# Two-layer diffusion backbone on one core: attention of layer 0 started without a barrier behind its projection, pooled products spread over neighbouring steps

## The reference, cut to what matters

```python
def mixer_ab(h, hc, w_in, w_out, pool_w, pool_scale, sink, cos, sin, need_ctx):
    u, q, k, v = split_ab(h @ w_in)              # 512 pooled channels, 8 query heads, 2 key/value heads
    uc, qc, kc, vc = split_ab(hc @ w_in)
    q, k = apply_rope(q, cos, sin), apply_rope(k, cos, sin)
    a = windowed_latent_attention(q, k, v, kc, vc, sink)
    y = jnp.concatenate([pool_mix(u, pool_w, pool_scale), a], axis=-1) @ w_out
    ...
def pool_mix(u, w, scale):                       # windows 2, 4, 8, 16, one per group of 128 channels
    ...
    d = (pooled - uf).astype(u.dtype)
    y = jnp.einsum('btgc,gce->btge', d, w).reshape(B, T, POOL_CH)
    return y * scale
```

## Time and profile before

| | us |
|---|---|
| median of 3 runs | 1578.04 (1577.26 to 1580.77) |
| the profiled execution | 1582.88, its span 1580.8 |
| PE busy | 1473.0 (93% of the span) |
| DVE busy | 966.0 (61%) |
| ACT busy | 716.3 (45%) |
| POOL busy | 596.6 (38%) |
| chain that ended last, share of PE | 83% |

### The profile page before, as it was taken

How to read it: one execution, slowest core, us unless ns; L and a number is a source line. 1 busy time by engine, 2 the same in 40 slices (tenths; PEclk the granted TensorE clock), 3 DMA queues, 4 the chain that set the end, 5 groups by cost and what they waited for, 6 DMA issues and landing times.

```text
span 1580.8 us, 22196 instructions
## 1 busy us (share of the span) xinstructions
PE 1473.0 (93%) x7604; PEld 1200.9 (76%) x7604; DVE 966.0 (61%) x1478; ACT 716.3 (45%) x1230; POOL 596.6 (38%) x529
## 2 busy tenths in 40 slices
PE   4989798999999999999999698899999999999997
PEld 1877466787888888887888577678877888887886
DVE  2447588567787668843345567788876544445455
ACT  2332466644332333223343545487775554443453
POOL 2251354352232232322333532375552444443454
PEclk9999799999999999999999899899999999999999
DMA  8230750123554346311121112110003233332332
GB/s 339 55 101 0 256 199 28 26 83 105 162 173 133 107 146 186 111 62 60 56 74 60 50 52 90 44 41 1 1 1 93 68 93 106 93 93 80 95 96 102
DMA packets 129034, 147.06 MB, mean 93 GB/s; under 512 B 7284, under 2 KB 95608, under 8 KB 127936
## 3 DMA queue, kind: packets, MB, share of 16 engines
q1 hardware_dynamic: 128960, 146.07, 29.5%
HBM read 143.92 MB, written 2.14 MB: 92 GB/s over the span
## 4 chain that ended last, share of the span: by engine, by line
PE 83%; DVE 7%; ACT 3%; POOL 2%; DMA 2%; issue 2%; SPq 0%; DVEq 0%; POOLq 0%; ACTq 0%
PE ps L471 23%; PE ps L472 23%; PE ps L473 23%; PE ps L1428 4%; PE ps L1414 3%; PE ps L1439 2%; PE ps L1441 2%; DMA ada_w<-in_ada_w_dram 1%; DMA start_w<-in_ada_w_dram 1%; PE ps L924 1%; POOL w_lo L463 1%; PE ps L1330 1%; DVE hT_lo L803 1%; ACT prob L1468 1%; DVE hT_hi L801 1%
## 5 line engine op out<-in xcount | busy, mean ns | idle before, releaser
L463 POOL TENSOR_TENSOR w_lo<-raw,w_hi 128x1024 fp32r<-128x1024 f32 (+1 forms) x183 | 346.5, 1896 | 618.0 <-ACT w_hi L456 618.0
L471 PE MATMUL ps<-hT_hi,w_hi 128*128 128x512 f32 (+1 forms) x1096 | 387.8, 354 | 9.3 <-DVE hT_lo L803 5.1
L472 PE MATMUL ps<-hT_lo,w_hi 128*128 128x512 f32 (+1 forms) x1096 | 385.3, 352 | 0.0
L473 PE MATMUL ps<-hT_hi,w_lo 128*128 128x512 f32 (+1 forms) x1096 | 382.9, 349 | 0.0
L456 ACT ACTIVATE w_hi<-raw 128x1024 fp32r<-128x1024 f32 (+1 forms) x200 | 173.0, 866 | 196.8 <-PE ps L473 166.5
L471 PEld LDWEIGHTS ps<-hT_hi,w_hi 128*128 128x128 f32 x1096 | 207.4, 189 | 47.1 <-DVE hT_lo L803 5.7
L473 PEld LDWEIGHTS ps<-hT_hi,w_lo 128*128 128x128 f32 x1096 | 206.8, 189 | 28.7
L472 PEld LDWEIGHTS ps<-hT_lo,w_hi 128*128 128x128 f32 x1096 | 207.3, 189 | 26.9
L2299 DVE TENSOR_TENSOR g_lo<-act_g,g_hi 128x768 fp32r<-128x768 f32 (+1 forms) x82 | 103.8, 1273 | 149.4 <-ACT g_hi L2258 149.0
L471 PE MATMUL ps<-w_hi,g_hi 128*128 128x512 f32 x410 | 160.2, 391 | 5.0 <-DVE g_lo L2299 4.5
L473 PE MATMUL ps<-w_hi,g_lo 128*128 128x512 f32 x410 | 159.6, 389 | 0.0
(11 more groups left out here) (242 smaller groups left out, 2433.3 us busy)
## 6 DMA issues: line engine op xcount, KB each, us to landing
raw<-in_ffn_w_up_dram SPq DMA_DIRECT2D x84, 512.0 KB, 3.9
ada_w_up<-in_ada_w_dram SPq DMA_DIRECT2D x48, 512.0 KB, 4.2
raw<-in_ffn_w_down_dram SPq DMA_DIRECT2D x84, 256.0 KB, 2.6
ada_w<-in_ada_w_dram SPq DMA_DIRECT2D x32, 512.0 KB, 4.9
start_w<-in_ada_w_dram SPq DMA_DIRECT2D x8, 1024.0 KB, 10.9
raw<-in_c_w_qkv_dram SPq DMA_DIRECT2D x12, 512.0 KB, 3.8
raw<-in_ab_w_in_dram SPq DMA_DIRECT2D x8, 512.0 KB, 5.0
raw<-in_ab_w_out_dram SPq DMA_DIRECT2D x8, 512.0 KB, 3.7
```

Of the source, the lines that this page charges most:

```text
L463: by.tensor_tensor(w_lo[:, slot, 0:width], raw[:, n % RAW, 0:width], w_hi[:, slot, 0:width].bitcast(F32), ALU.subtract).then_inc(lo_split, 1)
L471: nc.tensor.matmul(outp, s_hi, m_hi, start=first, stop=False, skip_group_check=True)
L472: nc.tensor.matmul(outp, s_hi, m_lo, start=False, stop=False, skip_group_check=True)
L473: return nc.tensor.matmul(outp, s_lo, m_hi, start=False, stop=last, skip_group_check=True)
```

## The change

1. The barrier between the two stages goes, on PE, ACT, DVE, POOL and SP. In its place stand the waits that the data need; SP waits for the last tile and for the fourth pooled product.
2. `pool_split` of windows 0 and 1 moves on DVE from behind tile 10 to behind tile 8, that of 2 and 3 from behind tile 11 to behind tile 10. On PE, products 0 and 1 move in front of the turn of tile 9. Scores S0 of group 0 go in front of the turn of tile 11, S1 behind it.
3. Products 2 and 3 become a step M in slot 0 of attention, their evictions a step m in slot 1. All A, H, P, Z, U, W and Y move two slots later (`POOL_FILLS`). A 0 also waits for the last pooled eviction.
4. d1 moves to memory that attention does not use at that time.

```diff
+POOL_FILLS = 2
...
-        at.setdefault(4 * (p // 3) + p % 3, []).append(("A", p, 0))
+        at.setdefault(POOL_FILLS + 4 * (p // 3) + p % 3, []).append(("A", p, 0))
...
-        at.setdefault(3, []).append(("H", 0, 0))
-        at.setdefault(7, []).append(("H", 1, 0))
+        at[0], at[1] = [("M", 2, 0), ("M", 3, 0)], [("m", 2, 0), ("m", 3, 0)]
+        at.setdefault(POOL_FILLS + 3, []).append(("H", 0, 0))
+        at.setdefault(POOL_FILLS + 7, []).append(("H", 1, 0))
...
+                        if l == 0 and n == len(tiles) - 2:
+                            pool_product(pe, 0)
+                            pool_product(pe, 1)
...
-            if l == 0:
-                pool_products((0, 1))
-            for late in range(n - TURN_LAG[l], n):
-                turn(late)
-            if l == 0:
-                pool_products((2, 3))
-            close(pe, "pe")
+            if l:
+                for late in range(n - TURN_LAG[l], n):
+                    turn(late)
+                close(pe, "pe")
+            return lambda: turn(n - 1)
...
+                        if l == 0 and n == len(tiles) - 1:
+                            pool_hi(act, 0)
...
-                if l == 0 and n == len(tiles) - 2:
+                if l == 0 and n == len(tiles) - 4:
                     pool_split(dve, 0)
                     pool_split(dve, 1)
+                if l == 0 and n == len(tiles) - 2:
+                    for f in (2, 3):
+                        dve.wait_ge(s("pool_mm"), f - 1)
+                        pool_split(dve, f)
             if l == 0:
-                for f in (2, 3):
-                    dve.wait_ge(s("pool_mm"), f - 1)
-                    pool_split(dve, f)
-                for f in range(4):
-                    pool_lo(dve, f)
-            close(dve, "dve")
+                pool_lo(dve, 0)
+            else:
+                close(dve, "dve")
...
-            after_phase(pe, before)
+            if l:
+                after_phase(pe, before)
...
+                    if kind == "M":
+                        pool_product(pe, g)
+                    elif kind == "A":
+                        if g == 0:
+                            pe.wait_ge(s("pool_out"), 16)
                         ada0_products(pe, g)
...
                     if h >= 2:
                         pe.wait_ge(s(f"exp_done{l}"), per * (h - 2) + 1)
+                    elif l == 0 and h == 0:
+                        pe.wait_ge(s("turned_read0"), rope_plan(0)[1][-2] - 2)
+                    elif l == 0:
+                        last_turn()
+                        pe.wait_ge(s("turned_read0"), rope_plan(0)[1][-1])
...
-                    after_phase(sp, 4)
+                    sp.wait_ge(s("acc_done0"), len(token_tiles(0)))
+                    sp.wait_ge(s("pool_mm"), 4)
                     ada0_sync(sp)
```

More of the change, by code:

```diff
@@ L976, in proj_tensor, with pool_product @@
                 m += 4
[L977 to L986, removed]
-            if l == 0:
-                pool_products((0, 1))
-            for late in range(n - TURN_LAG[l], n):
-                turn(late)
-            if l == 0:
-                pool_products((2, 3))
-            close(pe, "pe")
+            if l:
[3 more added lines that the diff above has]
+            return lambda: turn(n - 1)
+        def pool_product(pe, f):
+            pe.wait_ge(s("pool_d"), 2 * f + 2)
+            if f >= 2:
+                pe.wait_ge(s("pool_out"), 4 * (f - 1))
+            for v, (c0, w) in enumerate(STREAMS):
+                p0 = PADDED[v][0]
+                mm = mm3(bank(4 + 2 * (f % 2), 1024)[:, c0:c0 + w], pw_hi[:, f, :], pw_lo[:, f, :],
+                         d_hi[f % 2][:, p0:p0 + w], d_lo[f % 2][:, p0:p0 + w], True, True)
+            mm.then_inc(s("pool_mm"), 1)
         def proj_prefetch(l):
@@ L1092, in proj_scalar, with pool_hi @@
                     m += 1
+            if l == 0:
+                pool_hi(act, 1)
             for late in range(n - TURN_LAG[l], n):
                 read_turned(late)
-            if l == 0:
-                for f in range(4):
-                    act.wait_ge(s("pool_mm"), f + 1)
-                    for v, (c0, w) in enumerate(STREAMS):
-                        nc.scalar.activation(hT_hi[:, f, c0:c0 + w], bank(4 + 2 * (f % 2), 1024)[:, c0:c0 + w],
-                                             ACT.Copy, scale=cols[:, 48 + f:49 + f]).then_inc(s("pool_hi"), 1)
-            close(act, "act")
+            if l:
+                close(act, "act")
+        def pool_hi(act, f):
+            act.wait_ge(s("pool_mm"), f + 1)
+            for v, (c0, w) in enumerate(STREAMS):
+                nc.scalar.activation(hT_hi[:, f, c0:c0 + w], bank(4 + 2 * (f % 2), 1024)[:, c0:c0 + w],
+                                     ACT.Copy, scale=cols[:, 48 + f:49 + f]).then_inc(s("pool_hi"), 1)
         DIFFERENCE_AFTER = (0, 2, 7, 9)
@@ L1372, in ada0_columns, with attn_tensor @@
                                         ALU.mult).then_inc(s("gates_made0"), 1)
-        def attn_tensor(pe, l, before):
+        def attn_tensor(pe, l, before, last_turn=None):
             groups, steps, first = attn_setup(l)
@@ L1447, in attn_scalar @@
             groups, steps, first = attn_setup(l)
-            after_phase(act, before)
+            if l:
+                after_phase(act, before)
             for kind, g, i in steps:
-                if kind in "APZUWYHzu":
-                    if kind == "H":
+                if kind in "APZUWYHzuMm":
+                    if kind == "m":
+                        pool_hi(act, g)
+                    elif kind == "H":
                         out_split_hi(act, l, g)
@@ L1504, in attn_vector @@
             steps = outputs_first(steps)
-            after_phase(dve, before)
+            if l:
+                after_phase(dve, before)
+            else:
+                dve.wait_ge(s("qk_steps0"), rope_plan(0)[0][-1])
             nden = 2 if l == 0 else 1
@@ L1527, in attn_vector @@
                 if kind == "S":
+                    if l == 0 and h == 1:
+                        pool_lo(dve, 1)
                     dve.wait_ge(s(f"scores{l}"), h + 1)
@@ L2400, in _ @@
             for l in range(2):
-                b = 5 * l
+                b = 4 * l
                 norm_vector(dve, f"mix{l}", b + 2)
```

37 lines of the change are left out of this document (21 added, 16 removed).

## The result

The changed kernel takes 1582.71 us (median of 8 runs, 1579.63 to 1585.98), the kernel before beside it 1577.99. The ratio is 1.0027, with a 95% interval of 1.0015 to 1.0039: slower by about 4.3 us by the ratio (4.7 by the two medians), where 1576.7 was forecast. Run again word for word it took 1581.36 us, ratio 1.0017 (1.0004 to 1.0031). The loss is small, but there.

The account below looks back on a forecast made before the run. PE sets the pace to about 234 us, DVE for some 24 us, then PE; SP's ada_w request limits attention's start. 3.0 + 3.2 - 4.35 - 0.5 = 1.35 us less: 1576.7 us, range 1571 to 1582.

Parts of the forecast that it names:

- term 4: From group 6 to the end of attention: waits that go and come sum to 0.5 us lost.
- term 2: From the start of A 0 to the first turn of group 1: 3.2 us more won.
- The bound of 4.5 us lost: Groups 6 to the end: worst case, none of three old waits goes and both new ones come.
- a sign of being wrong: The forecast is wrong if groups 6 to 11 take over 3 us less or more than before.
- the end pays: Rival, end of attention: all three old waits go, 3.4 us won there, 1572.8 us in all; chance 0.23.
- Term 1: Start of attention: SP's ada_w loads go at 160.5 in place of 163.5, 3.0 us earlier.
- my first rival: The clock falls to half at the last projection turn: 2.3 us later, net 1 us lost, 1579.0; chance 0.15.
- Term 3: Ada pairs side by side: PE waits 1.3 us at A 5, A 8, A 11, A 14; 4.35 us lost.
- Slow load: Rival at A 5, A 8, A 11, A 14: tiles land after 6.2 us, net 8.25 lost, 1586.3; chance 0.12.
- POOL's splits: Rival at H 0 and H 1: PE pays 1.69 us twice, net 2.0 lost, 1580.1; chance 0.05.
- Renamed barrier: Rival, start of attention: SP still waits for four products and goes no earlier, 1579.7 us; chance 0.03.
- The offset: Whole kernel: median of runs 4.8 us below the profiled execution, subtracted to give the base of 1578.04 us.

Follow-up runs that it names:

- unpaired: The changed kernel with only the ada pairs moved so that no two stand side by side: 1574.58 us, ratio 0.9972; again 1573.94 us, ratio 0.9969.
- half-tile kernel: The changed kernel with each ada tile's load cut to 512 of 1024 columns, half the ada weights left out: 1577.34 us, ratio 0.9989.

## Why the prediction was wrong, point by point

**The step that failed is term 4, "0.5 us back", for groups 6 to the end.** It came to 2.6 us on the first traces and 4.1 on the second. From tile 8's turn to the last product the forecast was 1.35 us won and the traces have 1.9 and 4.5 lost; of the 3.3 and 5.9 us between, term 4 makes up 2.1 and 3.6. Its waits were summed nearly right: 9.4 us before (both traces), 10.0 after, 0.6 more, where I had 0.5. Those of W for its bank gave way to the 3.01 us at W 3 as foretold (3 us), W 0 waits 1.20 (1.5 foretold), the 1.87 us in the last group is gone.

Two things were not in it. First, ada work moved into the stretch: Z 0 came ahead of group 6's scores before and comes behind them now, 1.05 us. This is the other end of a slip in term 2, which took A 3's absence ahead of T as a gain (1.06 us) though A 3 only moves behind it. A moved step was counted where it left and not where it went.

Second, the clock: after the 3.0 us wait it fell in both traces of after, and in one of four others with the same end slots, three of six; it cost 2.6 us. After the 2.1 us wait of the old slots it fell in one trace of five, and cost 1.6 us. I had priced the longer wait at its own length alone. Six and five traces do not show that the fall is likelier after the longer wait, and it came after shorter ones too (1.2 us at W 0). The bound of 4.5 us lost held, but the second pair of traces passed the 3 us that the forecast gave as a sign of being wrong, and no rival was built on that end: I made "the end pays" a rival and left out "the end loses".

**Term 1, 3.0 us: right**, 3.7 by A 0 in the first traces. S 0 stood ahead of the last turn. The second trace of after had the half clock at the last turn (my first rival; so had both unpaired traces, three of the ten without the barrier): A 0 came 2.5 us later (2.3 forecast), but the clock was back sooner, and T stands where it stood.

**Term 2, 3.2 us: too large.** From A 0 to T it was 11.5 us before and 9.8 after, 1.7 us, of which 1.06 is A 3. The forecast had 8.3 us there, and what it had wrong is A 2. Its tile, asked for at 166.4, landed after 5.8 us and not after 4.5, so PE waited 1.13 us where none was forecast, and A 2 took 1.93 us at half clock. Both terms together gave 5.4 and 4.8 us, not 6.2.

**Term 3, 4.35 us back: right, a little small.** The stretch became 4.8 and 5.3 us longer. In the first trace there are four waits of 1.11 to 1.51 us, 4.93 us against 5.2 forecast, none at A 10. The loads asked for behind the pairs landed after 3.6, 3.6, 4.0 and 3.6 us (3.8 taken); 3.2 us, the estimate from the Trainium skill ("DMA: Bandwidth & Descriptors", Anatomy of one DMA), is lower than all four, and the trace decides. What I missed were three waits of 0.64 us for o_low; one of them stood there before (0.65), and two of before for prob (0.21 and 0.69 us) are gone.

**The other rivals.** Slow load: no, 4.0 us at most at those four places. POOL's splits: H 0 held a DVE instruction of one element for 1.77 us, about as in the earlier trace rows, and H 1 one of the D step for 2.31 us, nearly the 2.38 us of the split itself; PE did not wait behind either. Renamed barrier: no. So the kernel became slower without the mechanism that I had put on that side.

**The offset.** I took the profiled execution's 4.8 us over the median as one constant. 1.5 us of it and the half clock behind it were the late weights at 114 us, 2.6 us by tile 8's turn against the trace of after, and 1.6 us the half clock behind W 1's wait. The base of term 4 thus held a fall of the clock that four of the five traces with those end slots do not have at that place.

## What to carry to other kernels

When steps move by slots, list for each stretch what leaves it and what enters it, and look at which steps become neighbours: here, two slots put ada pairs side by side and Y 2 in front of W 3, and this alone cost 6.2 us, more than dropping the barrier brought. A step that waits for a ring of buffers to be refilled should stand with other work between its uses; here pairs apart turned the same change from 4 us lost to 4 us won. Before comparing two traces, find a common mark ahead of the change and count from there.

## What the runs showed of the hardware

- The granted clock after the same wait differs from one execution to the next: behind 3.01 us at W 3, matmuls of 0.63 us in one trace and 0.39 in another, worth 2.6 us of a stretch of 69. Behind the 1.2 us wait at W 0 it fell in four traces of eight, worth 1.1 us. The Trainium skill ("TensorE: Matmul & The Clock Gate", Part 1) says the same of the point at which the clock changes, that it varies from run to run; the traces agree.
- Halving a load did not halve its time: behind the first two ada steps that stand side by side, the two loads of 512 KB landed after a median of 4.1 us, and two of 256 KB, in the half-tile kernel, after 3.0.
- A GpSimd instruction of 2.4 us held a VectorE instruction of one element for 1.69 us in the kernel before, and for 1.77 and 2.31 us in the changed kernel.
- A load of 512 KB some 40 us ahead of the change landed after 4.6 to 5.0 us in seven of the fourteen traces and after 3.5 to 3.8 in the others. With the half clock behind it, this shifted one trace against another by 2.6 us, nearly as much as the effect looked for.
